# ScalarE sums squares for four norms, and one norm's weights are fetched during the experts

## The reference, cut to what matters

```
for l in 0, 1:
    h = mixer(x @ w_in[l]) @ w_out[l]
    x = layer_norm(a*x + h, ln_g[l,0], ln_b[l,0])
    h = cross_attention(x, mem)                      # ends in @ wo[l]
    x = layer_norm(a*x + h, ln_g[l,1], ln_b[l,1])    # the norm in front of the router
    h = experts(x, router)                           # 16 experts, 2 per token
    x = layer_norm(a*x + h, ln_g[l,2], ln_b[l,2])    # the norm behind the experts
h = rms_norm(x, mix_norm_g)                          # block 2's first norm
x = x + (gated sum of attention and a scan, from h @ w_in_2) @ w_out_2
x = x + experts_2(rms_norm(x, ffn_norm_g))
x = x + sigmoid(x @ w_ple_gate) * (p @ w_ple_proj)
out = rms_norm(x, final_norm_g)

layer_norm(y) = (y - mean(y)) * (var(y) + 1e-5)^-0.5 * g + b
rms_norm(y)   = y * (mean(y*y) + 1e-6)^-0.5 * g
```

## Time and profile before

| what | value |
|---|---|
| median of three runs | 1660.1 us (1658.19 to 1664.85) |
| the profiled execution, own time | 1664.57 us |
| its span, first to last instruction | 1662.8 us |
| mean granted TensorE clock | 0.966 |
| busy: PE, PEld, DVE, ACT, POOL | 93%, 78%, 77%, 67%, 3% |
| DMA | 422.75 MB, mean 254 GB/s over the span |

### The profile page before, as it was taken

One profiled execution on the slowest core, in us unless ns is written; L12 is line 12 of the kernel. 1 busy time (PEld: TensorE's weight loads), 2 busy tenths in 40 slices (PEclk: granted clock), 3 DMA queues, 4 the chain that ended last, 5 costly groups with the idle time before them and its releaser, 6 DMA issues.

```text
span 1662.8 us, 21036 instructions
## 1 busy us (share of the span) xinstructions
PE 1543.1 (93%) x8087; PEld 1296.8 (78%) x8087; DVE 1274.3 (77%) x1594; ACT 1119.2 (67%) x1340; POOL 57.2 (3%) x94
## 2 busy tenths in 40 slices
PE   7999988999997989998999998898998889999976
PEld 5788877888886778976788886787887778888855
DVE  4757458999997476447999998558655689999963
ACT  4544537999994644445999997267453479999952
POOL 5000000000001000000000000000000000000000
PEclk8999999999998999999999999999988999999988
DMA  9345427999996534534999998343533479999950
GB/s 330 124 164 202 152 102 271 391 392 392 393 395 249 173 134 170 204 125 153 377 391 393 393 395 334 121 152 102 172 132 98 162 249 388 392 393 395 394 194 26
DMA packets 176693, 422.75 MB, mean 254 GB/s; under 512 B 7052, under 2 KB 7216, under 8 KB 176576
## 3 DMA queue, kind: packets, MB, share of 16 engines
q1 hardware_dynamic: 172400, 407.92, 67.2%
q0 software_dynamic: 4176, 13.30, 2.4%
HBM read 420.15 MB, written 1.05 MB: 253 GB/s over the span
## 4 chain that ended last, share of the span: by engine, by line
PE 72%; DVE 16%; ACT 7%; issue 4%; DMA 1%; POOL 0%; POOLq 0%; ACTq 0%; DVEq 0%
PE ps L960 14%; DVE w_low L1652 11%; PE ps L986 7%; PE ps L675 5%; PE ps L676 4%; PE ps L680 4%; PE ps L997 4%; ACT w_high L1336 3%; PE ps L722 3%; PE ps L782 3%; PE ps L723 3%; PE ps L969 3%; PE ps L789 3%; PE ps L783 3%; PE ps L727 3%
## 5 line engine op out<-in xcount | busy, mean ns | idle before, releaser
L1652 DVE TENSOR_TENSOR w_low<-raw,w_high 128x1024 fp32r<-128x1024 f32 x588 | 693.9, 1222 | 253.3 <-ACT w_high L1336 250.1
L1336 ACT ACTIVATE w_high<-raw 128x1024 fp32r<-128x1024 f32 x588 | 598.2, 1055 | 334.7 <-PE ps L680 122.9
L986 PE MATMUL ps<-w_high,hT 128*128 128x512 f32 x384 | 154.0, 401 | 0.4
L986 PE MATMUL ps<-w_low,hT 128*128 128x512 f32 x384 | 153.2, 399 | 0.0
L960 PE MATMUL ps<-w_high,x_first 128*128 128x512 f32 x384 | 152.4, 397 | 0.3 <-ACT x_first L1389 0.2
L960 PE MATMUL ps<-w_low,x_first 128*128 128x512 f32 x384 | 150.2, 391 | 0.0
L675 PE MATMUL ps<-w_high,act_high 128*128 128x512 f32 x272 | 111.3, 409 | 6.4 <-DVE w_low L1652 3.6
L1652 DVE TENSOR_TENSOR w_low<-work,w_high 128x1024 fp32r<-128x1024 f32 x96 | 113.1, 1221 | 0.0
L676 PE MATMUL ps<-w_low,act_high 128*128 128x512 f32 x272 | 109.3, 402 | 0.0
L1652 DVE TENSOR_TENSOR w_low<-x_res,w_high 128x1024 fp32r<-128x1024 f32 x90 | 106.0, 1221 | 0.0
L680 PE MATMUL ps<-w_high,act_low 128*128 128x512 f32 x272 | 104.0, 395 | 0.0
(11 more groups left out here) (372 smaller groups left out, 3102.9 us busy)
## 6 DMA issues: line engine op xcount, KB each, us to landing
raw<-in_w_up SPq DMA_DIRECT2D x96, 1024.0 KB, 8.8
raw<-in_w_gate SPq DMA_DIRECT2D x51, 1024.0 KB, 9.0
raw<-in_w_down SPq DMA_DIRECT2D x48, 1024.0 KB, 8.6
work<-in_w_gate SPq DMA_DIRECT2D x45, 1024.0 KB, 8.7
x_res<-in_w_down SPq DMA_DIRECT2D x45, 1024.0 KB, 8.2
raw<-in_w_in SPq DMA_DIRECT2D x44, 1024.0 KB, 6.2
raw<-in_w_out SPq DMA_DIRECT2D x12, 1024.0 KB, 5.0
raw<-in_wk_x SPq DMA_DIRECT2D x8, 1024.0 KB, 5.0
```

The source lines that it names most:

```text
L986: i = pe.matmul(YS[:, b, :], hT[:, k, :], weights(u, 512 * b, 512 * b + 512)[half_w], start=(k + half_w == 0), stop=(k + half_w == FC))
L1336: A(split_unit(n)[0], raw_unit(n), ACT.Copy).then_inc(high_ready, 1)
L1652: V.tensor_tensor(split_unit(n)[1], raw_unit(n), split_unit(n)[0].bitcast(F32), ALU.subtract).then_inc(low_ready, 1)
```

## The change

- `branch_normed`: the sum with the residual also gives the sum over the row (`accum_out`), which is turned into minus the mean. VectorE centres and weighs into x; ScalarE at the same time squares the centred tile, with a sum over the row, into `junk` (GB). VectorE makes mean square plus epsilon from it, GpSimd the root, and VectorE the scale and shift. `bn_stats` and `bn_aggr` go. ScalarE's two squares stand behind its `split(8)` and in front of `routing_input`.
- `finished`: `norm_of_sums` takes the place of `layer_norm`. Tile 0 goes as before, but to its end before tile 1 begins. Of tile 1 ScalarE copies the sum out of PSUM with its row sum, makes minus the mean, and squares; VectorE centres, weighs, scales and shifts.
- `rms_norm` of block 2: ScalarE squares each tile after `normed`, and the weights lie in `mix_g` (GA). GpSimd fetches them in block l = 1 after expert 11's last gate-and-up unit, in front of its wait for the roots of the norm behind the experts; the fetch after that norm goes. The root, one instruction for both tiles before, becomes one for each.
- The counts of `idle`, the order of SP's loads and TensorE's list stay.

```diff
+        neg_mean, ssq = stat(632, TT, 1), stat(634, TT, 1)
+        mix_g = GA[:, 0:D]
+        junk = GB[:].rearrange("p (t n) -> p t n", t=TT)
...
 # GpSimd
                 for k in range(3):
+                    if 3 * l + k + 1 == 3 * DEPTH:
+                        wait_unit_used(pool, up_used(l, NE - QUAD - 1))
+                        pool.dma_start(mix_g, bcast(norms[3 * DEPTH][0], D)).then_inc(S["mix_loaded"], 16)
                     for t in range(TT):
                         root(rstd[:, t, :])
-                    load_norm(3 * l + k + 1)
-            root(rstd)
+                    if 3 * l + k + 1 < 3 * DEPTH:
+                        load_norm(3 * l + k + 1)
+            for t in range(TT):
+                root(rstd[:, t, :])
...
 # ScalarE
+            def squared(src, t, **centre):
+                A(junk[:, t, :], src, ACT.Square, accum_out=ssq[:, t, :], **centre).then_inc(S["ssq_ready"], 1)
+            def second_of_sums(m, src, arrived):
+                if arrived is not None:
+                    act.wait_ge(arrived, 2)
+                else:
+                    act.wait_ge(y_added[m], TT * NE)
+                chain.link(A(y_acc[:, 1, :], src, ACT.Copy, accum_out=neg_mean[:, 1, :]))
+                A(neg_mean[:, 1, :], neg_mean[:, 1, :], ACT.Copy, scale=-1.0 / D).then_inc(S["mean_ready"], 1)
+                act.wait_ge(S["mean_ready"], m + 1)
+                squared(y_acc[:, 1, :], 1, bias=neg_mean[:, 1, :])
...                                      # end of experts_own, after split(1)
+                if m < DEPTH:
+                    second_of_sums(m, flat(ps[:, 2 * SUM_SLOTS[1]:2 * SUM_SLOTS[1] + 2, :]), sums_done[m])
...
                 turned_high(act_high, (L + "oT0", L + "oT1"))
                 split(8)
+                for t in range(TT):
+                    act.wait_ge(S["centre_ready"], TT * l + t + 1)
+                    squared(summed[:, t, :], t, bias=neg_mean[:, t, :])
                 routing_input((L + "x2T0", L + "x2T1"), x, ALPHA)
...                                      # after experts(1)
+            for t in range(TT):
+                act.wait_ge(S["normed"], TT * (3 * DEPTH - 1) + t + 1)
+                squared(x[:, t, :], t)
             tiles_high(act_high, ("2.xT0", "2.xT1"))
...
 # VectorE
+            def squares_summed(t):
+                nonlocal sums_of_squares
+                sums_of_squares += 1
+                dve.wait_ge(S["ssq_ready"], sums_of_squares)
+                root_inverted(V.tensor_scalar(rstd[:, t, :], ssq[:, t, :], 1.0 / D, LN_EPS, ALU.mult, ALU.add))
+            def scaled(t):
+                root_ready()
+                V.scalar_tensor_tensor(x[:, t, :], x[:, t, :], rstd[:, t, :], norm_p[:, 1, :], ALU.mult, ALU.add).then_inc(S["normed"], 1)
+            def norm_of_sums(k, src, arrived):
+                dve.wait_ge(S["norm_loaded"], norm_need[k])
+                if arrived is not None:
+                    dve.wait_ge(arrived, 1)
+                for b in range(2):
+                    i = V.bn_stats(bn[:, 0, b, :], src[0][:, 512 * b:512 * b + 512])
+                link(i)
+                link(V.bn_aggr(mean_var[:, 0, :], bn[:, 0, :, :]))
+                root_inverted(V.tensor_scalar(rstd[:, 0, :], mean_var[:, 0, 1:2], LN_EPS, None, ALU.add))
+                link(V.scalar_tensor_tensor(x[:, 0, :], src[0], mean_var[:, 0, 0:1], norm_p[:, 0, :], ALU.subtract, ALU.mult))
+                scaled(0)
+                nonlocal means
+                means += 1
+                dve.wait_ge(S["mean_ready"], means)
+                link(V.scalar_tensor_tensor(x[:, 1, :], y_acc[:, 1, :], neg_mean[:, 1, :], norm_p[:, 0, :], ALU.add, ALU.mult))
+                squares_summed(1)
+                scaled(1)
             def branch_normed(k, names, scale):
                 for t in range(TT):
-                    add_branch_tile(names[t], t, summed, scale)
...
+                    add_branch_tile(names[t], t, summed, scale, neg_mean[:, t, :])
+                    V.tensor_scalar(neg_mean[:, t, :], neg_mean[:, t, :], -1.0 / D, None, ALU.mult).then_inc(S["centre_ready"], 1)
+                    centres += 1
+                    dve.wait_ge(S["centre_ready"], centres)
+                    link(V.scalar_tensor_tensor(x[:, t, :], summed[:, t, :], neg_mean[:, t, :], norm_p[:, 0, :], ALU.add, ALU.mult))
+                    squares_summed(t)
+                    scaled(t)
...
+            def rms_norm(src, dst):
+                dve.wait_ge(S["mix_loaded"], 16)
+                for t in range(TT):
+                    sums_of_squares += 1
+                    dve.wait_ge(S["ssq_ready"], sums_of_squares)
+                    root_inverted(V.tensor_scalar(rstd[:, t, :], ssq[:, t, :], 1.0 / D, RMS_EPS, ALU.mult, ALU.add))
+                    root_ready()
+                    V.scalar_tensor_tensor(dst[:, t, :], src[:, t, :], rstd[:, t, :], mix_g, ALU.mult, ALU.mult).then_inc(S["normed"], 1)
```

More of the change, by code:

```diff
@@ L509, in build @@
         for g, b in norms:
-            norm_need.append((norm_need[-1] if norm_need else 0) + (16 if b is None else 32))
+            apart = len(norm_need) == 3 * DEPTH
+            norm_need.append((norm_need[-1] if norm_need else 0) + (0 if apart else 16 if b is None else 32))
         block = ctx.enter_context(nc.Block())
@@ L1375, in experts @@
                 act.wait_ge(S["routed"], m + 1)
-                first = n
+                first = n, chain.n
                 with act.If(act.value_load(crowded[0:1, 0:1], min_val=0, max_val=1) == 0):
@@ L1379, in experts @@
                 assert n == moe_at[m][0] + UNITS * NE + SPLIT
-                n = first
+                n, chain.n = first
                 with act.Else():
@@ L1643, in _ @@
             turned = 0
-            roots = 0
+            roots = sums_of_squares = means = centres = 0
             def split(count):
@@ L1683, in root_ready, with layer_norm @@
                 dve.wait_ge(S["rstd_ready"], roots)
-            def layer_norm(k, src, centred, splits=0, arrived=None):
+            def layer_norm(k, src, centred, splits=0):
                 for t in range(TT):
-                    if arrived is not None:
-                        dve.wait_ge(arrived, t + 1)
                     for b in range(2):
@@ L1702, in branch_normed @@
             def branch_normed(k, names, scale):
+                nonlocal centres
                 dve.wait_ge(S["norm_loaded"], norm_need[k])
                 for t in range(TT):
-                    add_branch_tile(names[t], t, summed, scale)
-                    for b in range(2):
-                        i = V.bn_stats(bn[:, t, b, :], summed[:, t, 512 * b:512 * b + 512])
-                    link(i)
-                    link(V.bn_aggr(mean_var[:, t, :], bn[:, t, :, :]))
-                    root_inverted(V.tensor_scalar(rstd[:, t, :], mean_var[:, t, 1:2], LN_EPS, None, ALU.add))
@@ L1712, in branch_normed @@
-                    link(V.scalar_tensor_tensor(summed[:, t, :], summed[:, t, :], mean_var[:, t, 0:1], norm_p[:, 0, :], ALU.subtract, ALU.mult))
-                    root_ready()
-                    V.scalar_tensor_tensor(x[:, t, :], summed[:, t, :], rstd[:, t, :], norm_p[:, 1, :], ALU.mult, ALU.add).then_inc(S["normed"], 1)
+                    add_branch_tile(names[t], t, summed, scale, neg_mean[:, t, :])
+                    V.tensor_scalar(neg_mean[:, t, :], neg_mean[:, t, :], -1.0 / D, None, ALU.mult).then_inc(S["centre_ready"], 1)
@@ L1738, in add_branch, with add_branch_tile @@
                     add_branch_tile(name, t, dst, scale)
-            def add_branch_tile(name, t, dst, scale):
+            def add_branch_tile(name, t, dst, scale, total=None):
                 wait_full(dve, name)
-                frees(V.scalar_tensor_tensor(dst[:, t, :], x[:, t, :], scale, slot_ps(name), ALU.mult, ALU.add), name)
+                frees(V.scalar_tensor_tensor(dst[:, t, :], x[:, t, :], scale, slot_ps(name), ALU.mult, ALU.add, accum_out=total), name)
                 wait_released(dve, name)
@@ L1849, in experts @@
             def experts(m):
-                nonlocal n, turned, roots
+                nonlocal n, turned, roots, sums_of_squares, means
                 dve.wait_ge(S["routed"], m + 1)
-                begun = n, turned, roots, chain.n
+                begun = n, turned, roots, sums_of_squares, means, chain.n
                 with dve.If(dve.value_load(crowded[0:1, 0:1], min_val=0, max_val=1) == 0):
@@ L1858, in experts @@
                         split(1)
-                ended = n, turned, roots, chain.n
+                ended = n, turned, roots, sums_of_squares, means, chain.n
                 assert n == moe_at[m][0] + UNITS * NE + SPLIT
-                n, turned, roots, chain.n = begun
+                n, turned, roots, sums_of_squares, means, chain.n = begun
                 with dve.Else():
@@ L1868, in experts @@
                             V.tensor_copy(x[:, t, :], y_acc[:, t, :]).then_inc(S["moe_added"], 1)
```

(4 more changed lines are left out.)

15 lines of the change are left out of this document (5 added, 10 removed).

## The result

The changed kernel takes 1666.2 us (median of seven runs, 1664.98 to 1668.29), against 1662.55 for the kernel before (seven runs, 1658.19 to 1664.85). The ratio is 1.0028, with a 95% interval of 1.0016 to 1.0040: a small loss, under the 0.5% that was set as the bound. The forecast was 1663.0 us, on a median before of 1660.1 (three runs), in a range of 1657 to 1668. The profiled execution took 1666.33 (span 1664.6), 1.8 more than the profiled one of before, while the medians lie 3.65 apart. The two profiles are 4.1 apart at the turned tile in front of block 2; 2.3 of that comes back further on, in code that the change does not touch.

What follows compares the result with a forecast made beforehand. VectorE was taken to bound the experts, and a chain of waits from engine to engine the norms. Terms 2.0 + 0.4 + 0 + 0.5 = +2.9 us on a median of 1660.1 gave 1663.0 us, range 1657 to 1668.

Steps and rivals of the forecast that it cites:

- The squares stand behind `split(8)`: In front of the router, tile 0's square waits for the eighth split; tile 1's sum 2.0 (l = 0), 2.4 us (l = 1) later.
- squares not held: Rival: ScalarE free in front of the router, saving 1.05 us in l = 0 and 2.1 in l = 1; 1657.5 us, chance 0.08.
- Tile 1 alone, 3.62: In front of the router, an unhindered tile takes 3.62 us from sum to scale instead of 4.67, 1.05 less.
- The term of l = 0: In front of l = 0's router: held squares delay tile 1's sum and TensorE's unread products, +2.0 us; bounds -1.05 to 2.4.
- The term of l = 1: In front of l = 1's router: later second turned tile, +1.95 us, less 1.54 from high-clock router products; +0.4, bounds -2.1 to +2.0.
- nothing is given back: Rival: l = 1's router products stay at low clock (+2.0 us there), fetch paid whole (1.3); +5.3, 1665.4 us, chance 0.25.
- Behind the experts, 0: Behind the experts, both norm chains shorten, but TensorE's unread products end later; both terms 0, at most 0.1 us either way.
- The rival in which VectorE's end sets the start: Behind the experts, VectorE's shorter chains count, -0.8 and -3.6 us; total -1.5, 1658.6 us, chance 0.06.
- The fetch, +0.5: Early `mix_g` load in l = 1's experts: +0.5 us; 0 if slack takes it up, at most 1.33 of full DMA path.
- The table switch: Rival: table loads of 1.283 us around squares and router exponentials in two blocks, +5.1 on the forecast, 1668.1 us, chance 0.05.

Runs made afterwards that it cites:

- Experiment 1: Changed kernel with tile 0's square put in front of ScalarE's last three splits in front of the router: 1657.14 us, ratio 0.9976 to the kernel before.
- experiment 7: Changed kernel with tile 0's square before ScalarE's last three splits and fewer unread products behind the experts: 1645.49 us, ratio 0.9913 to the kernel before.
- experiment 2: Changed kernel with the old `branch_normed` (`bn_stats`, no squares) in front of the router: 1661.81 us, ratio 1.0011 to the kernel before.
- experiment 6: Kernel before with unread products behind the experts cut to 4 and 12 from 8 and 26: 1658.61 us, ratio 0.9995 to the kernel before.
- experiment 3: Kernel before with only the new `branch_normed` and its ScalarE squares in front of the router: 1663.95 us, ratio 1.0027 to the kernel before.
- experiment 4: Changed kernel with the early `mix_g` fetch made four times, ScalarE waiting for all: 1670.35 us, ratio 1.0065 to the kernel before.
- experiment 5: Changed kernel with unread products behind the experts cut to 4 and 12 from 8 and 26: 1654.92 us, ratio 0.9969 to the kernel before.

## Why the prediction was right, step by step

**The squares stand behind `split(8)`: right, to a tenth.** The square of tile 0 was to start with the end of the eighth split; it does. The sum of tile 1 comes 8.04 after that of tile 0 in l = 0, where it came 234.29 - 228.39 = 5.90, so +2.14 for the forecast's 2.0, and 8.39 in l = 1, +2.5 for 2.4. Experiment 1 shows the cause: with the splits put behind the square, nothing else changed, the delay is gone and the rival "squares not held" comes true in its mechanism. Its price is larger than that rival's: against before the stretches are 2.7 and 3.6 us shorter, where the rival had 1.05 and 2.1. With the pause at 2.50 TensorE stayed at the high clock in this execution, and the 14 records of l = 0 take 3.19 instead of the 3.66 of the earlier trace rows, which the rival left as they were; in that of experiment 7 it did not, and the stretch is 1.0 shorter than before, which is the rival's price. In l = 1 the router's products, too, run at the high clock.

**Tile 1 alone, 3.62: measured 3.60** in l = 0. The faster second tile gained nothing there, as forecast: it is ready at 241.6, and the 14 records end at about 245.6.

**The term of l = 0 is the one mis-sized: +2.0 forecast, +3.2 measured.** I carried the sum's delay to the end of TensorE's list and kept the list's own length. From the first of the 4 records to the transposes of tile 1 it was 242.10 - 235.56 = 6.54, and is 245.56 - 238.03 = 7.53: +1.0. This is no accident of two profiles: the stretch is 19.72, 19.48 and 19.52 in the three executions with the old norm (before, experiments 2 and 6) and 22.91, 22.80, 22.86 and 22.70 in the four with the squares behind the splits (changed kernel, experiments 3, 4 and 5). The delay itself lengthens TensorE's pause from 3.55 to 5.70, and after it TensorE runs at the lower level for longer. The same unread products that the kernel does to keep the clock up are what sets the end, so the low clock is paid in full. I had weighed what a longer pause does in l = 1 and not in l = 0, where I took the clock as before.

**The term of l = 1: +0.4 forecast, +0.5 measured, but half by luck.** The 14 records after the pause were to end at 758.35 - 752.55 = 5.8 after the sum of tile 1; the transposes behind them start 761.29 - 755.74 = 5.6 after it. The router's products got the high clock, as the forecast had it. But experiment 2 shows that the old code gets it too in another execution (18.03). Against that one the new stretch is +2.0, the rival "nothing is given back" in this term; against before and experiment 6 (19.51 and 19.58) it is +0.5 and +0.4. Over the three the term is +1.0, from a mean of 19.04 to 20.00 in the four executions of the new norm. The forecast took the low clock of its one profile for a property of the old kernel; that it was the commoner case of the three was luck.

**Behind the experts, 0: right.** The chains are shorter (from the first `bn_stats` to both tiles of block 2 ready, 1054.94 - 1043.25 = 11.69 for 1055.44 - 1039.98 = 15.46) and the unread products are not: in l = 0, TensorE does them to 535.87, 1.3 after the tiles, and in front of block 2 for 6 us more. The rival in which VectorE's end sets the start needs the cut of experiment 5. The one stretch that went down, l = 0's (11.32 to 9.74), did not come from the new norm, since experiment 3 with the old one has 9.65; the unread products take 5.12 in the changed kernel, with the clock at 0.50 for some 2.9 of it, and took 6.58 in the execution of before, with 5.8 of it at 0.50. In front of block 2 the stretch went up, 17.78 to 18.58, and that is the unread products again (14.40 for 13.18): with the same old norm there experiment 3 has 19.12.

**The fetch, +0.5:** the profiles agree with it, but it lies within what executions differ by. The profile of experiment 4, with 1.1 for each of three more, is near the upper bound of 1.33 as the price without slack; its ratio, with 2.0 each and a wide interval, neither confirms nor refutes it.

**The table switch did not come.** No `ACT_TABLE_LOAD` stands by any square of L1373, neither after the router's exponentials nor after the experts. The Trainium skill, page "ScalarE: Activation LUTs", section "Table sets: the hidden batching unit", says that a switch is paid when a function is in another set than the loaded one; here the trace shows none of the four switches, which by the figure of that page's section "What ACT_TABLE_LOAD costs" are an estimate of 10.6 us.

**The sum.** Forecast 2.0 + 0.4 + 0 + 0.5 = 2.9; by the two profiles, in order of time, 3.2 (in front of the router, l = 0), 0.1 (experts), -1.6 (behind them), 1.1 (mixer and attention of l = 1, unchanged code), 0.5 (in front of the router), -0.3 (experts with the fetch) and 0.8 (behind them), that is 3.8, and with the 0.3 by which the profile of after is late before all this 1061.83 - 1057.76 = 4.1. Of the other stretches 1.1 - 2.3 = -1.2 is where no line has changed; 2.2 of the 2.3 come from the profile of before, which takes 347.06 from the sum in front of block 2's second norm to the end, where the nine others take 344.6 to 345.0. Medians and ratio say 3.65 to 4.6 (0.0028 of 1660), and the terms over all executions say the same: 3.2 + 1.0 + 0 + 0.5 = 4.7. So the mechanism was right, and the sum was 0.75 to 1.8 too small, by the clock in l = 0 and in l = 1. The distance of 3.2 from 1663.0 to 1666.2 has a second part: 2.45 of it is that the median before was 1660.1 in three runs and 1662.55 in seven.

**What stays open.** What the fetch and the new norms behind the experts cost together: experiment 2 bounds it to -0.2 to +4 us. And the gain of experiment 5 by itself, 6 us by its stretch behind the experts: the ratio moved from 1.0028 to 0.9969, 9.8 us, and the rest of it is of the size of what the clock does further on from one execution to another (below).

## What to carry to other kernels

Before a piece of work goes to an idle engine, read the list of that engine at the place where it will stand: what waits in front of it holds it, however idle the engine is, and putting it three instructions earlier was worth 0.0052 of 1660, or 8.6 us, here. A delay in front of TensorE costs more than its own length when it then resumes at the low clock and filler work stands between it and the end. And filler sized for an old chain hides the gain of a shorter one: cut it in the same change.

## What the runs showed of the hardware that was not expected

**The root on GpSimd is slow beside one kind of VectorE operation.** Timeline of the kernel before: the root of tile 0, beside the centring of a tile, both of whose tensor inputs are in SBUF.

```profile
231.45 1.53 POOL L587 TENSOR_TENSOR stats<-stats,exponent 128x1 f32<-128x1 f32 x1 [82.87 <-DVE stats L1711]
```

Beside `bn_stats`, which reads one tensor, the same operation takes 0.56 in that kernel (1041.79). In the changed kernel VectorE waits for it and it takes 0.56; beside a centring that reads one tensor from PSUM, again 0.56:

```profile
1045.07 0.56 POOL L591 TENSOR_TENSOR stats<-stats,exponent 128x1 f32<-128x1 f32 x1 [83.10 <-DVE stats L1755]
```

The Trainium skill, page "SBUF — State Buffer", section "🔬 SBUF: two separate sides", says that a VectorE operation with two SBUF inputs and a GpSimd operation that reads SBUF exclude each other for a whole instruction. The traces agree: 1.53 is 0.56 and most of the centring's 1.27.

**The clock in block 2's scan.** One window of 10 us that begins 150 us after the turned tile in front of block 2, of the kernel before, of the changed one and of experiment 5. The code there is the same in all three.

```profile
1207.76:1217.76 10.00, 10.00 (x31) 7.53 (x30) 4.38 (x10) 4.42 (x4) 0.00 (x0) 0.66 0.34 107
```

```profile
1211.83:1221.83 10.00, 10.00 (x31) 7.57 (x30) 4.17 (x10) 4.38 (x4) 0.00 (x0) 0.66 0.30 108
```

```profile
1202.98:1212.98 10.00, 10.00 (x45) 8.09 (x44) 5.87 (x12) 5.39 (x5) 0.00 (x0) 1.00 0.33 107
```

TensorE is busy throughout in all three, yet the granted clock is 0.66 in two and 1.00 in the third, which gets through 45 records instead of 31. From the turned tile to block 2's norm in front of its router it takes 257.98, 257.91 and 254.22 us. In the ten profiled executions it takes 254.2 and 254.4 in experiments 5 and 1 and 257.6 to 260.2 in the others. That is as much as the whole effect of this change, and no edit was made there; what sets it was not found. The profiled execution of experiment 1 (1652.43) lies 4.7 under its median; that this clock is the reason is likely and not shown.
